# Two unused tiles of 64 bytes per partition are no longer allocated in a two-block transformer kernel

## The reference

```python
def first_block(x, ...):
    x = x + 0.5 * swiglu(rms_norm(x, ffn1_norm), ffn1_w_gate, ffn1_w_up, ffn1_w_down)   # 1024 -> 2816 -> 1024
    z = rms_norm(x, mix_norm) @ w_in + b_in                    # attention, mLSTM and gate inputs
    y_attn  = sliding_window_attention(...) @ w_proj_attn      # 16 heads of 64
    y_mlstm = (sigmoid(m_o) * rms_norm(mlstm_chunkwise(...))) @ w_proj_mlstm
    x = x + (gates[0] * y_attn + gates[1] * y_mlstm) @ w_out
    x = x + 0.5 * swiglu(rms_norm(x, ffn2_norm), ffn2_w_gate, ffn2_w_up, ffn2_w_down)
    return rms_norm(x, final_norm)

def second_block(x, mem, ...):
    h = x + concat(gated_linear_attention(...), latent_attention(...)) @ w_out
    h = h + cross_attention(rms_norm(h), rms_norm(mem)) @ xa_w_o
    fn = rms_norm(h, norm_ffn)
    return h + (silu(causal_conv3(fn @ ffn_w_gate)) * (fn @ ffn_w_up)) @ ffn_w_down
```

## Time and profile before

| | |
|---|---|
| three runs | 1015.22, 1017.05, 1020.97 us |
| profiled execution | 1020.97 us, of which the span is 1019.2 us |
| PE busy | 983.0 us, 96% |
| DVE busy | 690.5 us, 68% |
| ACT busy | 538.8 us, 53% |
| POOL busy | 101.8 us, 10% |
| read from HBM | 170.39 MB, 168 GB/s over the span |

### The profile page before, as it was taken

How to read it: one execution, slowest core, us unless ns; L and a number is a source line. 1 busy time by engine, 2 the same in 40 slices (tenths; PEclk the granted TensorE clock), 3 DMA queues, 4 the chain that set the end, 5 groups by cost and what they waited for, 6 DMA issues and landing times.

```text
span 1019.2 us, 20581 instructions
## 1 busy us (share of the span) xinstructions
PE 983.0 (96%) x8317; PEld 963.6 (95%) x8317; DVE 690.5 (68%) x1084; ACT 538.8 (53%) x779; POOL 101.8 (10%) x66
## 2 busy tenths in 40 slices
PE   5999999999999899999999999999989989999998
PEld 5999999998999799999999999999979889999997
DVE  5766765467779958766667646595666468888652
ACT  4554544345567964455544645485545564455431
POOL 1111110100000100011111104100001012223100
PEclk9999999999999999999999999999999999999999
DMA  8566675555554534565656764244235154665761
GB/s 243 181 190 199 202 232 176 171 169 162 167 166 129 162 125 159 172 225 189 206 168 203 233 206 125 93 136 154 84 98 172 62 180 152 199 203 174 256 199 42
DMA packets 168492, 172.33 MB, mean 169 GB/s; under 512 B 5604, under 2 KB 166894, under 8 KB 168302
## 3 DMA queue, kind: packets, MB, share of 16 engines
q1 hardware_dynamic: 165262, 170.57, 52.7%
q10 hardware_dynamic: 3168, 0.88, 0.5%
HBM read 170.39 MB, written 1.06 MB: 168 GB/s over the span
## 4 chain that ended last, share of the span: by engine, by line
PE 83%; DVE 5%; ACT 5%; issue 4%; DMA 1%; POOL 1%; SPq 0%; DVEq 0%; ACTq 0%; POOLq 0%
PE acc L657 75%; DVE wl L464 2%; DMA raw<-in_ffn_w_gate 1%; ACT wh L445 1%; POOL sq L2547 1%; PE part L994 1%; ACT L1397 1%; PE part L734 0%; PE part L710 0%; PE part L1193 0%; ACT prob L1336 0%; PE part L984 0%; ACT prob L1563 0%; PE part L782 0%; PE part L1175 0%
## 5 line engine op out<-in xcount | busy, mean ns | idle before, releaser
L445 ACT ACTIVATE wh<-raw 128x1024 fp32r<-128x1024 f32 (+3 forms) x298 | 319.6, 1098 | 296.9 <-PE acc L657 136.2
L657 PE MATMUL acc<-ah,wh 128*128 128x256 f32 x1520 | 429.2, 282 | 13.3 <-DVE al L1755 4.1
L464 DVE TENSOR_TENSOR wl<-raw,wh 128x1024 fp32r<-128x1024 f32 (+3 forms) x298 | 390.7, 1351 | 73.6 <-ACT wh L445 70.3
L657 PE MATMUL acc<-al,wh 128*128 128x256 f32 x1520 | 424.6, 279 | 0.0
L657 PE MATMUL acc<-ah,wl 128*128 128x256 f32 x1520 | 424.5, 279 | 0.0
L657 PEld LDWEIGHTS acc<-ah,wh 128*128 128x128 f32 x1520 | 289.2, 190 | 19.1 <-issue 7.9
L657 PEld LDWEIGHTS acc<-ah,wl 128*128 128x128 f32 x1520 | 289.3, 190 | 0.0
L657 PEld LDWEIGHTS acc<-al,wh 128*128 128x128 f32 x1520 | 289.2, 190 | 0.0
L657 PE MATMUL acc<-hh,wh 128*128 128x256 f32 x528 | 146.5, 277 | 0.0
L657 PE MATMUL acc<-hh,wl 128*128 128x256 f32 x528 | 146.4, 277 | 0.0
L657 PE MATMUL acc<-hl,wh 128*128 128x256 f32 x528 | 146.4, 277 | 0.0
(11 more groups left out here) (391 smaller groups left out, 1293.8 us busy)
## 6 DMA issues: line engine op xcount, KB each, us to landing
raw<-in_ffn_w_gate SPq DMA_DIRECT2D x33, 1024.0 KB, 5.3
raw<-in_ffn_w_up SPq DMA_DIRECT2D x33, 1024.0 KB, 5.3
raw<-in_ffn_w_down SPq DMA_DIRECT2D x24, 1408.0 KB, 6.3
raw<-in_w_in SPq DMA_DIRECT2D x33, 1024.0 KB, 5.3
raw<-in_w_out SPq DMA_DIRECT2D x8, 1024.0 KB, 5.1
raw<-in_w_proj_attn SPq DMA_DIRECT2D x4, 1024.0 KB, 5.1
raw<-in_w_proj_mlstm SPq DMA_DIRECT2D x4, 1024.0 KB, 5.5
raw<-in_xa_w_kv SPq DMA_DIRECT2D x4, 1024.0 KB, 5.2
```

The source lines that it names most:

```text
L445: nc.scalar.activation(wh[:, slot, a * nw:b * nw], raw[:, slot, a * nw:b * nw], ACT.Copy).then_inc(S("w_hi"), 1)
L464: nc.vector.tensor_tensor(wl[:, slot, a * nw:b * nw], raw[:, slot, a * nw:b * nw], f(wh[:, slot, a * nw:b * nw]), SUB).then_inc(S("w_lo"), 1)
L657: ins = mm(dst, a, b, start=st and q == 0, stop=en_ and q == 2, skip_group_check=True)
```

## The change

The allocations of the two unused tiles are taken out. Nothing else is changed.

```diff
         raw = sb("raw", [P, 2, SLAB])
-        half = sb("half", [P, 16])
         wh = sb("wh", [P, 2, SLAB], f32r)
         wl = sb("wl", [P, 2, SLAB], f32r)
-        rest = sb("rest", [P, 16])
         xT = sb("xT", [P, DC, T])
         xn = sb("xn", [P, DC, T])
         sq = sb("sq", [P, 4, 512])
```

## The result

The changed kernel takes 1047.65 us (median of 4 runs, 1044.15 to 1049.11), the kernel before 1018.2 us (4 runs): a ratio of 1.0285, 95% interval 1.0245 to 1.0325. It is slower, by 2.9%, where no change was forecast. In the later comparisons the kernel before had runs from 1015 to 1037 us, and the ratios leave out those that lie over 1.5% above its fastest, so they are a little unkind to kernels that have no such spread.

A forecast was written before the change was run, and what follows sets the result against it. It took PE's pace in long gapless matmul stretches as the bound. The terms summed to 1020.97 + 0 + 0 + 0 = 1020.97 us for the profiled execution, 1017.0 us for the median, no change; range 1011.5 to 1023.0.

The forecast's parts named there:

- Step (a): New tile starts modulo 256: zero for PE, bound 2.8 us either way on line 657's products; zero for ACT, 0.1 us.
- Step (b): Distance between raw and wh, read together by DVE at line 464: zero, bound 0.2 us either way.
- Step (c): Transfers with a new start (xraw, xn, memraw, two stores of res): zero, with 0.4 us to either side.
- The two paces: PE's long stretches run at about 113.5 or 117.8 ns a matmul, same code and clock; not due to tile places.
- rival 1: One of three fast long stretches falls to the slow pace, 117.8 ns: 4.6, 6.0 or 6.2 us slower; chance 7%.
- Rival 4: PE reads faster from rounder places in the long stretches: 26.7 us less, 990 us; chance 2%.

## Why the prediction was wrong

**What bounds the kernel** was read rightly: PE's pace in the long stretches. With PE as the bound, 5.3 ns on a matmul of 113.5 went into the time whole: 20.9 us of the chain in three stretches.

**Step (a) failed: "I take zero for PE".** Two things were wrong with its rows. The row compared tiles by their start, one at a time, and the cost lies in how the two operands of one instruction stand to each other. And it compared the length of a record, of transposes of 128 columns. That length is still 272 and 273 ns after the change, as in the earlier trace rows, so it says nothing of the slab products. Nor does a length give the pace: 281 ns stood at 117.8 ns for a matmul before and is the median at 118.9 now. The pace is in the counts, as the table of times had said, and there it rose by 5.3 of 113.5 ns, 4.7%, where the bound allowed 0.37%. So the bound was 2.8 us, and the span grew by 25.2. (Step (a) also took 1% of the chain for ACT, which is line 445 alone; all of ACT has 5%. It did no harm, since ACT did not get slower.)

The prediction's own signs caught it: the three long stretches were to stay at 113.5 ns, and a time of one instruction that moved by over 1% was to prove it wrong. PE's 276 ns became 281, 1.8%.

**Step (b)** asked the right question, a distance between two operands, of the wrong engine. It was right for DVE: line 462 is at 2.35 and 3.44 us and line 1835 at 684 ns. PE's own pair was never set down. The table of starts had what was needed: ah minus wh is 97984, 192 modulo 256, and 97920 after, 128.

**Step (c)** held: none of the four moved transfers was slower. The stores landed in 2.8 us instead of 2.9. The prediction's estimate from the Trainium skill's page "DMA: Bandwidth & Descriptors", section "How a descriptor splits into AXI transactions", was under 0.1 us. No run bears it out: memraw moved by 0.3 us and xraw by 0.3, so 0.1 can't be told from chance.

**The two paces and rival 1.** The prediction saw them and concluded "It isn't the place of tiles", since hh with wh had both. That excludes the place as the only cause, and not as one: the place sets which paces exist, and something that was not found picks one. Rival 1 had the sign, and for one stretch nearly the price (6 us against 7.4); all three fell, and to 118.9 ns, slower than the slow pace known. Rival 4, that PE's reads hang on places, was the right mechanism with the sign reversed, and at 2%.

The Trainium skill's page "SBUF — State Buffer", section "Who interferes with whom", gives PE two independent reading ports, one for each operand, and says that PE waits for no one. The prediction used another section of that page for the zero of step (b), and never put the question for PE's own two operands. The run of matmuls alone, at 113.4 to 120.1 ns by the distance of the two operands, shows that their addresses are not independent in what they cost, and the measurement decides.

## What to carry to other kernels

Where PE is the bound and each product loads its weights, try the two operands' addresses modulo 256 as a tuning parameter: here, in steps of 32 bytes, fp32r products of 128x128 by 256 columns cost 113.4 to 120.1 ns by that alone. Before an unused tile is called dead, work out for each engine on the path how the operands of one instruction stand to each other before and after. And a kernel whose runs spread by 2% at one clock may be sitting on a distance with two paces; look for counts per window that differ between stretches of the same code.

## What the runs showed of the hardware

- With nothing else at work, the pace was 120.0 ns at distance 0 modulo 256, 116.7 or 117.9 at 32, 113.4 or 117.9 at 64, 114 at 112, 118.7 or 120 at 128, 117.4 or 118.7 at 160, and 113.5 or 117.9 at 192, with the stationary operand at a multiple of 32. Distances off a multiple of 16 were at 116.7 to 123.5, and once at 129.7.
- At distance 112 the stationary operand's start mattered too: 113.5 to 114.0 ns at a multiple of 32, 120.1 ns 16 bytes off it, and 121.7 to 122.5 at 4 or 8 bytes off.
- What picks one of two paces was not found. The same stretch of 396 took 46.66 us in both traces at 192 and in the one at 64, which speaks against mere chance; breaks of four lengths did not order it. Nor was the reason for 256 bytes tried, or any other shape or type of operand.
